# An encoder layer in split fp32: work moved at the stage borders, and a new slot order in the mixer

## Chip, cores and metric

The kernel runs on one core of one Trainium2 chip. The metric is the device time of one execution in microseconds; the time before is the median of three runs. Engines: PE is TensorE (matrix products), DVE is VectorE, ACT is ScalarE, POOL is GpSimd, SP is the engine that issues most DMAs.

## What is computed

One layer of a streaming encoder on 1088 tokens (1024 of a prompt, 64 of a sample with caches), width 1024, all in fp32:

```python
x = x + 0.5 * swiglu_ffn(x, *ffn1)              # rms norm, 1024 -> 2 x 2816 -> 1024
h = rms_norm(x, mix_g)
o_a, o_b, state = mixer(h)                      # projections, two kinds of attention
x = x + merge_branches(h, o_a, o_b, *merge_w)   # gates, two projections, one out
x = x + 0.5 * swiglu_ffn(x, *ffn2)
x = x + per_layer_embedding(x, pe, *ple)        # "PLE"
```

Branch a of the mixer attends over a band of chunks, with a bias by relative position looked up in a table, and a sink for each head. Branch b attends causally with a decay: the scores of a query and a key get the difference of cumulative sums of log_sigmoid(forget gate). The forget gates are 8 columns of the projection.

## The kernel before

Every product is made of three: an operand is split into a high part (rounded by ACT, names in `_hi`) and a low part (the difference, subtracted by DVE or POOL, names in `_lo`), and PE adds hi x hi, lo x hi and hi x lo in PSUM (`three`, L674 for most). So a piece of weights goes DMA (`_raw`), ACT (`_hi`), DVE (`_lo`), PE.

Everything is written out by hand: each engine has its own program, engines meet at semaphores, and an instruction waits for all that stands ahead of it on its engine.

- **Prologue.** SP loads x. ACT squares the first half's tiles (L1400), PE sums them over partitions (`first_stats`, L773), ACT takes roots (`half_roots`, L1131), DVE inverts (`half_inverse`, L1517) and makes the operands (`operand_step`: `b_raw` L1528, then `h_lo` and `b_lo`, L1536 and L1539, behind ACT's `operand_hi`, L1139 to L1142). The position biases go another way: PE looks the table up (`rel_table_rows`, L764), ACT copies it (`table_rel`, L1403) and writes it to memory (`rel_by_position`, L1405), and SP loads it again in eight pieces, `rel_rows` (L2134).
- **FFN.** The tokens are taken in two passes of 544. A pass has 11 groups of hidden columns. Its first two groups are plain products, in pieces of 128x512 (`plain_hi` L616, `plain_lo` L621), the other nine go in pairs by a Strassen scheme: POOL's `combine` (L1966 to L1977) makes sums of weight blocks, `block_hi` (L602) and `block_lo` (L610) split them, and `differences` on DVE (L1545 to L1550) makes the matching sums of operands once a pass. `gate_part` and `other_part` on DVE (`steps`, L1579 to L1605) put the quarters together. `group_out` multiplies by the out weights (`out_hi` L635, `out_lo` L639: w_hi and w_lo, 128x1024), and DVE adds to x (`add_half`, L1612). Between head and last group a loop runs 8 periods of about 33 us.
- **The norm of the second half** is prepared while the first pass runs: ACT squares its 8 tiles (`half_square`, L1197), POOL sums them (`half_sums`, L1988), both in the head of the pass.
- **Border to the mixer (or to PLE).** Norms are applied in chunks of 364, 364 and 360 tokens, in `NORM_ORDER` (`norm_hi` L1109, `norm_lo` L1488), between the additions of the last group; the next stage's weights are split by `split_lo` (L588).
- **Mixer.** After a first pair of units (`unit_pair`), `mix` runs slots: 6 dense ones, then one for each of 76 attention items (20 of branch a, 56 of branch b). `unit_products` (L902) are the projections, 24 products of 128x364 for a unit and chunk; `scores` (L932), `turns` (L951: probabilities are transposed on PE) and `values_product` (L975) belong to an item, and run in different slots: `LAG` sets how many slots lie between an item's scores and its turn, and its values follow one slot later. ACT's `exponents` (L1345), `copies` (`probs_t`, L1294) and `outputs` (`o_t`, L1359) and DVE's row maxima (`neg_top`, L1771) and weights lie between. `log_forget` (ACT L1363 to L1368, DVE L1806 to L1817) turns forget gates into cumulative sums. `head_sums` (L993) and `turned_values` (L1005) serve norms of heads and values.
- **Merge.** Four groups, each with `unit_out` (outputs (m, c): tile m, token chunk c); the last feeds the norm of FFN2 (`merge_sums` on POOL, L1999).

The heart of a mixer slot on PE:

```python
scores(g, ...)
unit_products(taken, taken + todo // 2)
values_product(g, ...)
head_sums(slot, use[1])
unit_products(taken + todo // 2, taken + todo)
turns(TURN_AT[slot])
turned_values(slot, use[2], use[3])
```

## Time and profile before

| | |
|---|---|
| time, median of 3 runs | 2606.1 us (2605.12 to 2611.69) |
| the profiled execution | 2604.11 us, span 2602.4 us |
| mean granted clock of PE | 0.987 |
| busy: PE, DVE, ACT, POOL | 2525.6, 1817.5, 1011.1, 778.8 us |
| FFN1, both passes | about 20 to 795 us of the span |
| mixer, merge | about 795 to 1300, 1300 to 1694 us |
| FFN2, PLE | about 1694 to 2470, 2470 to 2602 us |

Times in the profile are microseconds from the span's start. "Busy" is time in which an engine executes; "idle before" stands in brackets behind an instruction, with what ended it. PEclk is the clock granted to PE, 1.00 at full speed.

### The profile page before, as it was taken

What the parts mean: (1) busy time and instruction counts of PE and PEld (TensorE: products, weight loads), DVE (VectorE), ACT (ScalarE), POOL (GpSimd) and SP (SyncE); (2) the same over time, 40 slices, a digit from 0 to 9 for tenths busy, and PEclk for the clock granted to TensorE, in tenths of its full rate; (3) what the DMA queues carried; (4) which work ended last, traced back from release to release, by engine and by line L of the source; (5) the groups of instructions that cost most, each with busy time, mean ns of one, the idle gap of its engine ahead of it and who ended that gap; (6) DMA issues with size and microseconds to landing.
All of it is one profiled execution on the core that took longest, in us unless ns stands there. A gap on an engine that the chain in (4) does not pass through costs nothing.

```text
span 2602.4 us, 47124 instructions
## 1 busy us (share of the span) xinstructions
PE 2525.6 (97%) x18062; PEld 2374.9 (91%) x18062; DVE 1817.5 (70%) x3345; ACT 1011.1 (39%) x1911; POOL 778.8 (30%) x628
## 2 busy tenths in 40 slices
PE   7999999999998899999999999989999999999899
PEld 7999999999998787777789889889999899999899
DVE  6688888788878676555433434487888777888764
ACT  5333343333335675555421111243333333333431
POOL 2355541455443000111100000234554224555410
PEclk8999999999999999999999999999999999999999
DMA  4222222222224101221121111122222222222112
GB/s 178 97 89 91 98 86 94 91 92 94 98 72 147 56 30 34 68 72 46 43 109 41 42 41 48 57 74 90 98 98 91 80 82 98 98 98 98 66 41 93
DMA packets 61846, 209.39 MB, mean 80 GB/s; under 512 B 7968, under 2 KB 10440, under 8 KB 61536
## 3 DMA queue, kind: packets, MB, share of 16 engines
q1 hardware_dynamic: 61408, 206.64, 22.2%
q8 instruction: 144, 2.36, 0.4%
q14 instruction: 38, 0.31, 0.0%
q10 hardware_dynamic: 256, 0.08, 0.0%
HBM read 192.11 MB, written 16.15 MB: 80 GB/s over the span
## 4 chain that ended last, share of the span: by engine, by line
PE 90%; DVE 6%; ACT 2%; issue 1%; DMA 0%; POOL 0%; DVEq 0%; ACTq 0%; POOLq 0%; SPq 0%
PE psum L674 68%; PE psum L902 9%; PE psum L1064 5%; PE psum L932 2%; PE psum L975 2%; PE psum L951 2%; PE psum L993 1%; DVE w_lo L639 1%; DVE rstd L1517 1%; DVE h_lo L1488 0%; DVE x L1612 0%; DVE w_lo L588 0%; DVE rstd L1495 0%; DVE b_raw L1528 0%; PE psum L773 0%
## 5 line engine op out<-in xcount | busy, mean ns | idle before, releaser
L674 PE MATMUL psum<-hid_hi,w_hi 128*128 128x272 f32 (+2 forms) x1536 | 451.7, 294 | 4.9 <-DVE hid_lo L1510 4.9
L674 PE MATMUL psum<-hid_lo,w_hi 128*128 128x272 f32 (+2 forms) x1536 | 451.8, 294 | 0.0
L674 PE MATMUL psum<-hid_hi,w_lo 128*128 128x272 f32 (+2 forms) x1536 | 451.2, 294 | 0.0
L674 PE MATMUL psum<-h_hi,gate_hi 128*128 128x272 f32 x1200 | 351.1, 293 | 27.2 <-DVE b_lo L1536 12.6
L674 PE MATMUL psum<-h_hi,other_hi 128*128 128x272 f32 x1200 | 351.5, 293 | 13.9 <-DVE other_lo L610 13.9
L674 PE MATMUL psum<-h_hi,other_lo 128*128 128x272 f32 x1200 | 350.4, 292 | 0.0
L674 PE MATMUL psum<-h_hi,gate_lo 128*128 128x272 f32 x1200 | 349.8, 292 | 0.0
L674 PE MATMUL psum<-h_lo,other_hi 128*128 128x272 f32 x1200 | 348.7, 291 | 0.0
L674 PE MATMUL psum<-h_lo,gate_hi 128*128 128x272 f32 x1200 | 348.2, 290 | 0.0
L1612 DVE SCALAR_TENSOR_TENSOR x<-psum,x 128x272 f32<-128x272 f32 x736 | 290.9, 431 | 59.1 <-PE psum L674 57.8
L674 PEld LDWEIGHTS psum<-hid_hi,w_hi 128*128 128x128 f32 x1536 | 289.2, 188 | 6.6 <-issue 6.3
L2004 POOL TENSOR_TENSOR hid_lo<-prod,hid_hi 128x272 fp32r<-128x272 f32 x160 | 140.3, 903 | 501.8 <-ACT hid_hi L1167 342.7
L674 PEld LDWEIGHTS psum<-hid_lo,w_hi 128*128 128x128 f32 x1536 | 290.1, 189 | 0.4
L674 PEld LDWEIGHTS psum<-hid_hi,w_lo 128*128 128x128 f32 x1536 | 289.6, 189 | 0.0
L674 PEld LDWEIGHTS psum<-h_hi,gate_hi 128*128 128x128 f32 x1200 | 228.3, 190 | 28.8 <-DVE gate_lo L621 10.2
L674 PEld LDWEIGHTS psum<-h_hi,other_hi 128*128 128x128 f32 x1200 | 229.3, 191 | 14.9 <-DVE other_lo L610 14.9
L674 PEld LDWEIGHTS psum<-h_lo,other_hi 128*128 128x128 f32 x1200 | 229.7, 191 | 0.0
L674 PEld LDWEIGHTS psum<-h_hi,other_lo 128*128 128x128 f32 x1200 | 229.2, 191 | 0.0
L674 PEld LDWEIGHTS psum<-h_lo,gate_hi 128*128 128x128 f32 x1200 | 228.8, 191 | 0.1
L674 PEld LDWEIGHTS psum<-h_hi,gate_lo 128*128 128x128 f32 x1200 | 228.4, 190 | 0.0
L610 DVE TENSOR_TENSOR other_lo<-other_raw,other_hi 128x1024 fp32r<-128x1024 f32 (+1 forms) x144 | 213.7, 1491 | 0.0
L674 PE MATMUL psum<-h_hi,w_hi 128*128 128x364 f32 (+1 forms) x576 | 193.7, 336 | 5.7 <-DVE h_lo L1488 3.8
(224 smaller groups left out, 5560.5 us busy)
## 6 DMA issues: line engine op xcount, KB each, us to landing
w_raw<-w_units SPq DMA_DIRECT2D x149, 512.0 KB, 3.2
gate_raw<-w_units SPq DMA_DIRECT2D x88, 512.0 KB, 4.2
other_raw<-w_units SPq DMA_DIRECT2D x88, 512.0 KB, 4.2
x<-x_t SPq DMA_DIRECT2D x16, 272.0 KB, 6.8
x_saved<-x SPq DMA_DIRECT2D x8, 544.0 KB, 6.1
x<-x_saved SPq DMA_DIRECT2D x8, 544.0 KB, 7.9
y_out<-x SPq DMA_DIRECT2D x8, 544.0 KB, 4.6
f_keys<-f_cumulative SPq DMA_DIRECT2D x4, 1024.0 KB, 6.6
```

Source lines behind the costliest of these rows:

```text
L610: dve.tensor_tensor(pair_lo[slot][:, first:first + n, :], pair_raw[slot][:, first:first + n, :], pair_hi[slot][:, first:first + n, :].bitc ...
L639: dve.tensor_tensor(w_lo[:, j, :], w_raw[:, j, :], w_hi[:, j, :].bitcast(F32), ALU.subtract).then_inc(out_lo_done, 1)
L674: mm = pe.matmul(out, w, m, start=first and n == 0, stop=last and n == 2)
L902: mm = pe.matmul(psum[:, x % 2, 0:width], (w_hi, w_hi, w_lo)[way][:, slot, k * P:(k + 1) * P], (h_hi, h_lo, h_hi)[way][:, k, c0:c0 + width ...
L932: mm = pe.matmul(psum[0:rows, SC[h], at:at + width], q[hb:hb + HD, part["b"] * P:part["b"] * P + rows], keys, start=True, stop=True)
L951: mm = pe.transpose(out, cols, ident[0:rows, 0:rows])
L975: mm = pe.matmul(psum[hb:hb + HD, PV, col:col + rows], vals[0:width, hb:hb + HD], probs_t[0:width, h, j * P:j * P + rows], start=first, st ...
L993: pe.matmul(psum[:, ST, 0:n], blocks, head_sq[:, r % 2, 0:n], start=True, stop=True).then_inc(head_sum_full, 1)
L1064: mm = pe.matmul(psum[:, ev.mod(BANKS), 0:n], w_raw[:, slot, (4 * br + k) * P:(4 * br + k + 1) * P], o_t[:, 4 * br + k, c0:c0 + n], start= ...
L1517: dve.reciprocal(rstd[:, c0:c0 + HN], rstd[:, c0:c0 + HN]).then_inc(half_rstd_done, 1)
L1612: dve.scalar_tensor_tensor(x[:, m, c0:c0 + HN], bank(e + n), half, x[:, m, c0:c0 + HN], ALU.mult, ALU.add).then_inc(psum_free, 1)
L2004: pool.tensor_tensor(part(lo, n), part(prod2, n), part(hi, n).bitcast(F32), ALU.subtract).then_inc(hid2_lo_done, 1)
```

## The change

1. **Prologue.** ACT loads the table of square roots ahead of the inputs by a dummy root. The table look-up moves behind the statistics on PE; the copy `table_rel` moves among the operand copies on ACT, and the write `rel_by_position` behind the last of them. `plain_lo` is done in two parts, behind operand steps 0 and 4.
2. **Heads.** The 8 squares and sums of the second half move from the head into the loop's periods (two in the first, one in each of six more), on ACT and POOL; their loops are unrolled in pass 0.
3. **Last pair of a pass.** Its second combine moves from POOL to DVE, ahead of `gate_part`; out weights of the last two groups use three slots and are split behind `block_lo`.
4. **Borders.** `NORM_ORDER` and the places of `norm_lo` and `split_lo` among the 32 additions change; at the mixer's and PLE's start three `inverse` go ahead of the reads.
5. **Mixer slots.** Scores, values and turns stand ahead of the unit products; lags grow from 1 to 2 (a) and 2 to 3 (b).
6. **Forget gates.** Their 8 low columns are copied beside the 8 high ones, so one product serves hi x hi and hi x lo; 16 instead of 24 products for a chunk, and the halves are added on DVE.
7. **Merge.** Outputs of groups 0 to 2 come in the order (0,0), (0,1), (1,0), (1,1), (0,2), (1,2) and on; in the last group the weights of FFN2 are split earlier, and the first three operand steps lie among the additions.

```diff
-LAG = {"a": 1, "b": 2}
+LAG = {"a": 2, "b": 3}
...
-NORM_ORDER = [(m, 0) for m in TILE_ORDER[:5]] + [(m, c) for m in TILE_ORDER[:5] for c in (1, 2)] + \
-    [(m, c) for m in TILE_ORDER[5:] for c in range(NCH)]
+NORM_ORDER = [(0, 0), (1, 0), (0, 1), (0, 2), (2, 0), (1, 1), (1, 2), (5, 0), (2, 1), (2, 2), (6, 0)] + \
+    [(m, c) for m in (5, 6) for c in (1, 2)] + [(m, c) for m in TILE_ORDER[5:] for c in range(NCH)]
...
+OUT_SLOTS = {2: (1, 2), 1: (0, 1)}
...
             def unit_products(q0, q1):
...
+                    both = MIX_UNITS[n][0] == "f"
+                    if both and way == 2:
+                        continue
...
             def mix():
...
-                    unit_products(taken, taken + todo // 2)
                     if slot in VALUE_AT:
...
+                    if slot in TURN_AT:
+                        turns(TURN_AT[slot])
+                    unit_products(taken, taken + todo // 2)
...
-                    if slot in TURN_AT:
-                        turns(TURN_AT[slot])
...
             def ffn(stage):
-                def period(number, group, e):
+                def period(number, group, e, tiles=()):
...
+                    for m in tiles:
+                        half_square(number, m)
...
-                    if t == 0:
-                        for m in range(4):
-                            half_square(number, m)
                     plain_sigmoid(group, e)
-                    if t == 0:
-                        for m in range(4, KD):
-                            half_square(number, m)
...
+            act.wait_ge(set_up, 2)
+            act.activation(eps_root[:], eps[:], ACT.Sqrt)
...
             for k in range(KD):
                 operand_hi(0, k)
+                if k == 1:
+                    act.wait_ge(table_full, 1)
+                    act.activation(table_rel[:], psum[0:8, 5, 0:REL], ACT.Copy, scale=-1.0).then_inc(table_done, 1)
+            act.wait_ge(table_done, 1)
+            act.dma_start(rel_dram, table_rel[:]).then_inc(table_out, 16)
             act.wait_ge(table_out, 16)
...
-                    out_lo(dve, At(last - 1), 0)
-                    out_lo(dve, At(last - 1), 1)
+                    sq = strassen_pair(At(2 * last + 1), number)
+                    dve.wait_ge(combined, 4 * sq.base)
+                    combine(dve, sq, At(last), 1)
                     gate_part(At(last), number, At(el))
                     for n in range(4):
                         block_lo(dve, At(2 * last + 1), number, 1, n)
+                    out_lo(dve, At(last - 1), 0, 2)
+                    out_lo(dve, At(last - 1), 1, 2)
+                    out_lo(dve, At(last), 0, 1)
...
-                norm_lo(norm, 0)
-                split_lo(dve, At(follower["u"]), At(follower["s"]))
-                norm_lo(norm, 1)
-                done = 2
-                for n in range(16):
-                    add_half(1, At(el + 30), n, 0.5)
...
+                done = 0
+                for n in range(32):
+                    add_half(1, At(el + 14 + 16 * (n // 16)), n % 16, 0.5)
+                    if n == 14:
+                        out_lo(dve, At(last), 1, 1)
+                    if n == 23:
+                        split_lo(dve, At(follower["u"]), At(follower["s"]))
+                    if n in (12, 20, 26, 29):
                         norm_lo(norm, done)
                         done += 1
...
+            def f_low_beside(n):
...
+                dve.tensor_copy(hi, lo).then_inc(f_beside, 1)
...
             def mix(e):
+                for c in range(NCH):
+                    inverse(0, c)
                 for c, (c0, n) in enumerate(CH):
-                    inverse(0, c)
                     read_scaled(k0[:, c0:c0 + n], e + c, c, 0)
...
             half_inverse(0)
             for n in range(len(OPERAND_STEPS)):
                 operand_step(0, n)
-                if n == 1:
-                    plain_lo(dve, 0, 0)
+                if n in (0, 4):
+                    plain_lo(dve, 0, 0, range(n // 2, n // 2 + 2))
```

ACT in the prologue, the kernel before: the table's copy and its write stand between the squares of the statistics, and a table load stands ahead of the roots.

```order
L1400 ACT_TABLE_LOAD
...
L1400 ACTIVATE sq_a<-x 128x544 [waits x_in0_1]
...
L1403 ACTIVATE table_rel<-psum 8x384 [waits table_full]
L1405 DMA rel_by_position<-table_rel 8x384 [waits table_done]
L1400 ACTIVATE sq_a<-x 128x544 [waits sq_a_read,x_in0_6]
...
L1131 ACT_TABLE_LOAD [waits half_stat_full]
...
L1131 ACTIVATE rstd<-psum,eps 128x272 [waits half_stat_full]
```

The same in the changed kernel, from the roots on (`h_hi` and `b_hi` are the operand copies):

```order
L1165 ACTIVATE rstd<-psum,eps 128x272 [waits half_stat_full] x2
L625 ACTIVATE gate_hi<-gate_raw 128x512 [waits gate_in]
...
L1438 ACTIVATE table_rel<-psum 8x384 [waits table_full]
...
L1176 ACTIVATE h_hi<-b_raw 128x2x272 [waits scaled] x4
L1440 DMA rel_by_position<-table_rel 8x384 [waits table_done]
L625 ACTIVATE other_hi<-other_raw 128x512 [waits other_in,table_out]
```

The write has moved behind all operand copies, and ACT waits for its end before it copies the next weights; the second table load is gone from here. SP's order is the same in both kernels: the `rel_rows` loads wait for that write, and the out weights stand behind them.

DVE at the border of a pass, before and then in the changed kernel (`other_raw` holds the weight blocks that are combined, `steps` and `gate` the quarters):

```order
L1517 RECIPROCAL rstd<-rstd 128x272 x2
L639 TENSOR_TENSOR w_lo<-w_raw,w_hi 128x1024 x2
L1579 TENSOR_TENSOR steps<-steps,psum 128x272
...
L1597 TENSOR_TENSOR gate_130<-gate_130,prod_131 128x272 x4
L610 TENSOR_TENSOR other_lo<-other_raw,other_hi 128x1024 x3
...
L621 TENSOR_TENSOR gate_lo<-gate_raw,gate_hi 128x512 x4
```

```order
L1548 RECIPROCAL rstd<-rstd 128x272 x2
L662 TENSOR_TENSOR other_raw<-other_raw 128x512
...
L1610 TENSOR_TENSOR steps<-steps,psum 128x272
...
L1628 TENSOR_TENSOR gate_130<-gate_130,prod_131 128x272 x4
L619 TENSOR_TENSOR other_lo<-other_raw,other_hi 128x1024 x3
...
L655 TENSOR_TENSOR w_lo<-w_raw,w_hi 128x1024 x3
L631 TENSOR_TENSOR gate_lo<-gate_raw,gate_hi 128x512 x4
```

Four combinations (one is shown) stand where two w_lo stood, and three w_lo now stand between other_lo and gate_lo.

PE in the mixer, one slot before and one in the changed kernel (`k`, `q`: scores; `probs_t`: values; `probs`: turns; `w_hi`, `w_lo`: unit products, of which the first is shown):

```order
L932 MATMUL psum<-k_98,q_97 128x256 x4
L902 MATMUL psum<-h_lo,w_hi 128x360
...
L975 MATMUL psum<-probs_t,v_tok_102 64x128 x8
L993 MATMUL psum<-head_sq,consts 128x364
L902 MATMUL psum<-h_hi,w_hi 128x364
...
L951 MATMUL psum<-consts,probs 128x128 x8
```

```order
L966 MATMUL psum<-ak_t,q_97 64x128 x2
L966 MATMUL psum<-k_98,q_97 64x64 x2
L1009 MATMUL psum<-probs_t,v_tok_102 64x128 x8
L985 MATMUL psum<-consts,probs 128x128 x8
L936 MATMUL psum<-h_hi,w_lo 128x364
...
L1027 MATMUL psum<-head_sq,consts 128x364
L936 MATMUL psum<-h_lo,w_hi 128x364
```

Values and turns have moved ahead of all products of the slot.

## Rows read from the trace of the kernel before

**Rows 1.** The page: busy time by engine, and one line of its DMA part.

```profile
PE 2525.6 (97%) x18062; PEld 2374.9 (91%) x18062; DVE 1817.5 (70%) x3345; ACT 1011.1 (39%) x1911; POOL 778.8 (30%) x628
...
w_raw<-w_units SPq DMA_DIRECT2D x149, 512.0 KB, 3.2
```

**Rows 2.** Windows: length, busy PE, PEld, DVE, ACT, POOL; clock, DMA share, GB/s.

```profile
20.00:55.00 35.00, 26.31 (x193) 26.12 (x194) 29.76 (x46) 20.61 (x38) 12.12 (x8) 0.89 0.38 130
55.00:350.00 295.00, 295.00 (x2331) 295.00 (x2331) 245.41 (x408) 108.86 (x175) 147.51 (x104) 0.99 0.26 92
...
1020.00:1300.00 280.00, 278.37 (x2004) 213.70 (x2002) 147.60 (x412) 150.83 (x350) 38.37 (x68) 1.00 0.17 55
...
1680.00:1730.00 50.00, 39.84 (x277) 39.23 (x278) 39.48 (x63) 25.52 (x44) 14.06 (x11) 0.91 0.18 64
...
1727.90:1731.00 3.10, 3.10 (x14) 3.10 (x15) 3.10 (x7) 3.10 (x6) 0.46 (x1) 0.50 0.02 5
```

**Rows 3.** Waits of PE: line, releaser; us in total, times, longest.

```profile
PE psum L674 <- DVE other_lo L610: 13.9, 4, 4.0
...
PE psum L1005 <- ACT v_tok L1308: 3.5, 1, 3.5
...
PE psum L932 <- DVE neg_top L1771: 2.1, 1, 2.1
PE psum L993 <- DVE k L1504: 2.0, 1, 2.0
...
PE psum L902 <- DVE q L1724: 1.7, 1, 1.7
PE psum L975 <- ACT probs_t L1294: 1.6, 3, 0.7
```

**Rows 4.** Timeline of PE: start, us, instruction, [idle before, its releaser]; prologue and heads.

```profile
9.46 0.81 PE L764 MATMUL psum<-onehot,table 32*8 32x384 f32 x2
...
24.05 0.57 PE L674 MATMUL psum<-h_hi,gate_hi 128*128 128x272 f32 x1 [9.81 <-DVE b_lo L1536]
...
54.78 0.39 PE L674 MATMUL psum<-h_hi,gate_hi 128*128 128x272 f32 x1 [4.63 <-DVE gate_lo L621]
...
1727.86 0.59 PE L674 MATMUL psum<-h_hi,gate_hi 128*128 128x272 f32 x1 [5.13 <-DVE gate_lo L621]
```

**Rows 5.** Timeline of ACT, prologue.

```profile
13.87 1.28 ACT L1131 ACT_TABLE_LOAD   x1 [1.23 <-PE psum L773]
15.17 0.86 ACT L1131 ACTIVATE rstd<-psum,eps 128x272 f32<-128x272 f32 x2
...
31.55 0.66 ACT L1142 ACTIVATE h_hi<-b_raw 128x544 fp32r<-128x544 f32 x1 [0.67 <-DVE b_raw L1528]
```

**Rows 6.** Timeline of DVE: heads, pass borders, a lone w_lo.

```profile
20.76 2.49 DVE L621 TENSOR_TENSOR gate_lo<-gate_raw,gate_hi 128x512 fp32r<-128x512 f32 x4
...
42.22 4.60 DVE L639 TENSOR_TENSOR w_lo<-w_raw,w_hi 128x1024 fp32r<-128x1024 f32 x2 [2.20 <-ACT w_hi L635]
46.74 2.44 DVE L1545 TENSOR_TENSOR t_raw<-b_raw 128x1088 f32<-128x1088 f32 x1
49.11 1.28 DVE L1546 TENSOR_TENSOR t_raw<-b_raw 128x1088 f32<-128x1088 f32 x1
...
398.62 1.23 DVE L639 TENSOR_TENSOR w_lo<-w_raw,w_hi 128x1024 fp32r<-128x1024 f32 x1
...
1715.31 2.29 DVE L639 TENSOR_TENSOR w_lo<-w_raw,w_hi 128x1024 fp32r<-128x1024 f32 x1 [2.44 <-ACT w_hi L635]
...
2040.20 4.21 DVE L639 TENSOR_TENSOR w_lo<-w_raw,w_hi 128x1024 fp32r<-128x1024 f32 x2
```

**Rows 7.** Timeline of SP's queue, prologue.

```profile
15.87 5.04 SPq L2134 DMA_DIRECT2D rel_rows<-rel_by_position  x8
```

**Rows 8.** DMA issues up to 60 us: count, KB each, us to landing.

```profile
w_raw<-w_units SPq DMA_DIRECT2D x2, 512.0 KB, 7.7
```

**Rows 9.** Window of the mixer's dense slots, unit products (L902) alone.

```profile
846.00:853.00 7.00, 6.68 (x36) 6.05 (x36) 1.00 0.01 2
```

More of the change, by code:

```diff
@@ L102 @@
 PRODUCTS = 3 * KD
+F_LOW = 32
 def attention_items():
@@ L616, in plain_hi, with plain_lo @@
                 act.activation(pair_hi[slot][:, b, :], pair_raw[slot][:, b, :], ACT.Copy).then_inc(pair_hi_done, 1)
-        def plain_lo(dve, group, slot):
-            for n, b in enumerate(PLAIN_BLOCKS):
+        def plain_lo(dve, group, slot, part=range(4)):
+            for n in part:
+                b = PLAIN_BLOCKS[n]
                 dve.wait_ge(pair_hi_done, 4 * (2 * group + slot) + n + 1)
@@ L720, in unit_pair, with unit_out @@
                         stats(norm, STAT_STEPS[step])
-            def unit_out(u, s, e, rows, h_count):
+            def unit_out(u, s, e, rows, h_count, order=tuple((m, c) for m in range(4) for c in range(NCH))):
                 pe.wait_ge(w_lo_done, (s + 1).v)
@@ L848, in pair, with group_out @@
                     mm.then_inc(psum_full, 1)
-            def group_out(group, e, hi, lo):
+            def group_out(group, e, hi, lo, ahead=0):
                 for j in range(2):
+                    slot = OUT_SLOTS.get(ahead, (0, 1))[j]
                     pe.wait_ge(out_lo_done, 2 * group + j + 1)
@@ L1262, in ffn @@
                     if t == 0:
-                        out_hi(act, At(last), 0)
-                        operand_hi(number + 1, 0)
-                        out_hi(act, At(last), 1)
-                        for k in range(1, KD):
+                        out_hi(act, At(last), number, 1, 1)
+                        act.wait_ge(psum_full, el + 30)
+                        for k in range(KD):
                             operand_hi(number + 1, k)
@@ L1373, in mix @@
                 for slot in range(N_SLOTS):
-                    if slot - 1 in TURN_AT:
-                        copies(TURN_AT[slot - 1])
+                    if slot in VALUE_AT:
+                        outputs(VALUE_AT[slot])
+                    if slot in TURN_AT:
+                        copies(TURN_AT[slot])
                     late, use = ST_AT.get(slot - 1), ST_AT.get(slot)
@@ L1384, in mix @@
                         head_root(use[1])
-                    if slot in VALUE_AT:
-                        outputs(VALUE_AT[slot])
                     for n in range(3, len(MIX_UNITS)):
@@ L1647, in ffn @@
                         head_gains()
-                    out_lo(dve, At(group), 0)
-                    out_lo(dve, At(group), 1)
+                    for j in range(2):
+                        out_lo(dve, At(group), j)
                     differences(number, e)
@@ L1680, in ffn @@
                     for n in range(16):
+                        add_half(t, At(el + 14), n, 0.5)
+                    for n in range(16):
                         add_half(t, At(el + 30), n, 0.5)
-                        if n == 5:
-                            out_lo(dve, At(last), 1)
+                        if n == 2:
+                            out_lo(dve, At(last), 1, 1)
                         if n % 2:
@@ L1926, in _ @@
                         split_lo(dve, u + 1, s + 1)
+                    if half == m == 0:
+                        for c in range(NCH):
+                            inverse(1, c)
                     for c, (c0, n) in enumerate(CH):
-                        if half == m == 0:
-                            inverse(1, c)
                         read_scaled(ple_gate[:, m, c0:c0 + n], e + c, c, 1 if half == m == 0 else None)
@@ L2007, in ffn, with period @@
             def ffn(stage):
-                def period(number, group):
-                    combine(group.times(2) + 1, number, group, 1)
-                    combine((group + 1).times(2), number, group + 1, 0)
+                def period(number, group, tiles=()):
+                    sq = strassen_pair(group.times(2), number)
+                    combine(pool, sq + 1, group, 1)
+                    combine(pool, sq + 2, group + 1, 0)
+                    for m in tiles:
+                        half_sum(number, m)
                     hidden2_lo(group, quarter, hid2_hi, hid2_lo)
@@ L2104, in ffn @@
                     el = e + E_LAST
+                    ev, where = el - E_PERIOD, at + 16 + 6 * (LOOP - 1)
+                    sp.wait_ge(psum_full, ev + 7)
+                    load_pair(0, At(where))
+                    if t == 0:
+                        sp.wait_ge(sum_b_done, KD * (stage["first"] // 2 + 1))
+                    load_out(1, At(where + 5), OUT_SLOTS[2][1])
+                    sp.wait_ge(psum_full, ev + 15)
+                    load_out(0, At(at + U_FFN - 2), OUT_SLOTS[1][0], last_in)
+                    sp.wait_ge(psum_full, ev + 23)
+                    load_out(0, At(where + 4), OUT_SLOTS[2][0])
+                    sp.wait_ge(psum_full, ev + 30)
+                    load_pair(1, At(where + 1))
                     sp.wait_ge(psum_full, el + 7)
```

212 lines of the change are left out of this document (109 added, 103 removed).

## The prediction

> **What bounds the kernel now.** I read the page first: TensorE (PE) is busy for 2525.6 of 2602.4 us, 97% [rows 1], so a change pays only where it removes PE idle time, PE work, or PE time at the lower clock. Then the windows by stage: in the loop of a feed-forward stage (FFN) PE is busy for all of 295.00 us, and in the settled mixer, 1020 to 1300, for 278.37 of 280 [rows 2]. Those have nothing to give. The two FFN heads have: 26.31 of 35 and 39.84 of 50 us, with a granted clock of 0.89 and 0.91 where a loop has 0.99 [rows 2]. The waits of PE say for whom it stands: other_lo, v_tok, neg_top, q, k, probs_t [rows 3] and, at the heads, b_lo and gate_lo [rows 4]. The clock I price from a row: in the 3.10 us behind the wait that ends at 1727.86 it is 0.50, the 1.2 of 2.4 GHz [rows 2, 4]; half of such a stretch, some 1.6 us, is lost beside the wait itself.
>
> The sum is made against the profiled execution, 2604.1 us, which lies 2.0 below the median of 2606.1. A measurement can tell about 0.3% (7.8 us) from no change.
>
> **1. Prologue and head of FFN1: 3.4 us gained, bounds -0.7 and 9.6.** ACT loads a table for 1.28 us between the last statistics product and the roots [rows 5]; the load moves ahead of the inputs, where ACT waits anyway: 1.28. Two table products, 0.81 us, leave PE's queue ahead of the statistics [rows 4]: 0.8. DVE subtracts four weight pieces in 2.49 us before the first operand [rows 6]; two of them now go later: 1.2. So PE starts at 24.05 - 3.3 = 20.8.
>
> But the head ends at another wait: PE stands for 4.63 us until 54.78, for gate_lo [rows 4], which DVE reaches after two out-weight subtractions (w_lo), 4.60, four differences, 2.44 for the first and 1.28 for each after it, and then the gate_lo themselves [rows 6]. POOL's sums of squares ran beside the first three of these; a lone w_lo takes 1.23 us [rows 6], so each loses 1.07 there. With the sums moved into the loop the chain shortens by 2 x 1.07 + 1.16 = 3.3, and the start by 3.3 as well: the wait could go whole, 3.3 + 4.63 + 1.6 of clock = 9.5, and with a tenth for ACT's shorter queue 9.6, the upper bound.
>
> I don't take it, for what is moved on a queue. The table of biases by position, whose copy and write ACT issued between two squares, now leaves behind ACT's last operand copy, which ended at 31.55 + 0.66 = 32.2 [rows 5] and would end 3 us sooner, near 29. SP, which waits for it, issued eight rel_rows loads from 15.87 on, in 5.04 us [rows 7], with the out weights behind them. Before, SP was let go at 15.87; now at 29 plus the write, for which I count between 2 us and the 5 that a load took under traffic: 32. Then the out weights are issued at 37 and land, at 3.2 us [rows 1] to 7.7 [rows 8], between 40 and 45; ACT rounds them in 1 us each and DVE starts w_lo at about 43, where it started at 42.22 [rows 6]. From there 2.5 (two w_lo) + 5.1 (four differences) + 1.9 (three of four gate_lo) gives 52.5; as the differences need no weights but stand behind w_lo, nothing overtakes. With loads at 42 it is 51.4, my value (the lower landing time is that of 149 such loads): 3.4 gained on 54.78. If they land last, 55.5: 0.7 lost.
>
> On the table load the Trainium skill (ScalarE: Activation LUTs, "What ACT_TABLE_LOAD costs") gives another price: 1283 ns and a drain of some 1380 ns more at each switch. Here the roots begin at 15.17, 0.02 us after the load's end [rows 5]; by the page the forecast would be 1.4 us lower, and I go by the row.
>
> **2. Head of FFN2: 6.7 gained, bounds 3 and 7.5.** The same chain without rel_rows: PE waits 5.13 us until 1727.86 [rows 4], and DVE's w_lo start at 1715.31, at 2.29 for one [rows 6], behind an ACT that squares four tiles first. Without the sums the w_lo save 2.1 and the first difference 1.16; without ACT's four squares, at the 0.66 that a copy of the same 128x544 takes at most [rows 5], the start saves about 2.2 (they overlap a little): 5.5 against 5.13. So the wait just goes, with its 1.6 of clock. The margin is small; half a wait left gives the lower bound.
>
> **3. Pass borders: 0.4 in FFN1, 2.5 in FFN2 (bounds 0 and 5).** DVE takes reciprocals, then two w_lo (4.21 us at 2040.20 [rows 6]), then the steps for which PE waits. The change puts four 128x512 combinations there, at the 0.62 of a gate_lo piece (2.49 / 4 [rows 6]) some 2.6 to 2.9 with their order kept, and w_lo behind other_lo's subtractions: 1.3 off the steps of FFN2, half a microsecond at FFN1, where the two ran shorter. The wait for other_lo that follows (of the four, 13.9 us [rows 3], two lie here) moves along. In FFN2 both waits lie close and share a slow stretch, of which I give back 1.2.
>
> **4. FFN1 to the mixer, 1.3 (bounds 0 and 6); FFN2 to the last stage, 3.5 (0 and 6).** The other two waits for other_lo, nearly 4 us each [rows 3], lose 0.5 by a combine on DVE instead of POOL. Behind them lie short waits for x, w_lo and h_lo. The order spreads h_lo among the additions, but DVE's work there remains: I keep most of the waits at the first border and drop half at the second.
>
> **5. Mixer start: 3.3 gained, bounds 0 and 7.** The 2.0 for k [rows 3] goes, as three reciprocals precede the reads. The forget gates take 16 products a chunk instead of 24: 24 fewer at 6.68 us for 36 [rows 9], 4.4. Against it: the early items wait for v_tok 3.5, neg_top 2.1 and q 1.7 [rows 3], where ACT and DVE work through the forget gates' logarithm and scans. Values and turns at the slot's head meet these chains with half a slot less of products in front: I count 4.2 + 0.6 + 4.0, 1.5 more, and one more slow stretch, 1.6. What is added for the forget gates (a copy, a longer addition) runs on DVE beside products.
>
> **6. Settled mixer, tail and merge: 0.5.** PE's only waits there are 1.6 us in three for probs_t [rows 3], at the tail, where no products are left: 0.2. The lag grows by one slot while values move up by half of one, so a chain has half a slot more than before. Of the reordered merge outputs the first two stay in place, and so the wait for the second's input: 0. The last merge group overlaps more of the next norm: 0.3.
>
> **Sum:** 3.4 + 6.7 + 0.4 + 2.5 + 1.3 + 3.5 + 3.3 + 0.5 = 21.6. 2604.1 - 21.6 = 2582.5; with the 2.0 to the median **2584.5 us**.
>
> **The rivals.**
> - *More goes than I count, 0.17.* The out weights land before DVE needs them (9.6 for 3.4), and the two borders out of the FFN hide their waits (5 more): 21.6 + 6.2 + 5 = 32.8, **2573**. For it: 3.2 us to landing on a free queue. Against: SP's 5.04 us of issue.
> - *The borders don't move, 0.15.* DVE bounds them, and another order of its work changes which output is late, not the last. Then 4.4 of products, 5 of FFN2's head, 2 of the prologue and 1 remain: 12.4, **2594**.
> - *POOL's sums hurt in the loop, 0.05.* If each of eight sums costs a DVE subtraction beside it what a w_lo loses, 1.07, a pass loses 8.6, and two 17 of the 21.6: **2601**. It decides only where DVE is just in time; over the loop it is busy for 245.41 of 295 [rows 2]. The Trainium skill (GPSIMD Engine Reference, "8. Key points") says that GpSimd shares its SBUF interfaces with VectorE, in contention with instructions of two SBUF inputs; by that rule the sums charge DVE wherever they are put, and the trace agrees for w_lo.
> - *Slower: the slot heads of the mixer wait, 0.05.* Turn, ACT's copy, value product: if this chain sets the pace, each of 76 item slots waits as the tail does, 1.6 / 3 = 0.54 [rows 3]: 41 us, **2625**. It decides from 21.6 / 76 = 0.28 us a slot. Against: the third slot of lag.
>
> **How the numbers follow.** My sum has 0.58, the rivals the rest. The range reaches from past the first rival, one border more, 2568, to past the second, with half of FFN2's head, 2598. Faster by over 0.3% means below 2598.3: my sum, the first rival and nearly all of the second, 0.87; within 0.3% 0.08, the third and the second's end; slower 0.05.
>
> **What would show it.** Right: no PE wait near 1722 and no slow stretch behind it; still some 4 us of waiting for gate_lo before the third group of FFN1, now near 51, with the out weights issued near 37; 24 fewer forget products; waits of about 4 us at the first value items. Wrong: PE waits in each slot after 1020, waits for other_lo above 4 us, idle time in the loops.

## The result, and the profile after

| | before | after |
|---|---|---|
| median of the runs, us | 2607.96 (2605.12 to 2611.69, 4 runs) | **2567.09** (2566.22 to 2568.53, 4 runs) |
| after / before | | **0.9843** [0.9826, 0.9860] |
| profiled execution, us | 2604.11 | 2568.53 |
| its span, us | 2602.4 | 2566.7 |

The gain is 40.9 us by the medians, where 21.6 were forecast, and the time lies 0.9 us below the range. Between the two profiled executions it is 35.7 on the spans: that of before ran 3.9 under its median, that of after 1.4 over. The parts below are counted on the spans.

The page of after, busy time by engine [rows 1]. The unit products are 24 fewer, and PE's busy time fell by 21.6 us:

```profile
PE 2504.0 (98%) x18038; PEld 2364.9 (92%) x18038; DVE 1797.5 (70%) x3362; ACT 1010.5 (39%) x1912; POOL 768.9 (30%) x612
```

Where the span was shortened, by landmarks on PE's timeline: the first product after the wait in question, for the mixer its first unit product (823.21 before, 819.81 after), and for the pass border of FFN2 the end of the last product ahead of it. The lengths and the busy time of PE are those of windows between the landmarks:

| stretch | before, us | after, us | gain | PE idle, before to after |
|---|---|---|---|---|
| start to first FFN1 product | 24.05 | 21.91 | 2.1 | |
| to the third group of FFN1 | 30.73 | 32.53 | -1.8 | 4.6 to 6.0 |
| to the pass border's end (other_lo) | 321.08 | 319.74 | 1.3 | 5.2 to 4.0 |
| to the first unit product of the mixer | 447.35 | 445.63 | 1.7 | 9.0 to 7.1 |
| to the first merge product | 477.54 | 463.02 | **14.5** | 11.6 to 12.8 |
| to the first product of FFN2 | 396.07 | 395.30 | 0.8 | 10.2 to 9.4 |
| to the pass border of FFN2 | 345.13 | 338.31 | 6.8 | 5.1 to 0 |
| over this border | 8.82 | 5.81 | 3.0 | 6.0 to 4.0 |
| to the end | 551.63 | 544.45 | 7.2 | 14.3 to 11.3 |

The fifth row is the surprise: the mixer gained most, and PE stands idle *longer* there than before, although the wait for k (2.0 of the 11.6) is gone from it.

Windows of after, in the columns of [rows 2] (the last one is the stretch behind the wait for v_tok):

```profile
20.00:55.00 35.00, 27.08 (x194) 26.86 (x195) 25.61 (x45) 16.97 (x29) 0.00 (x0) 0.84 0.42 137
55.00:350.00 295.00, 295.00 (x2335) 295.00 (x2334) 241.99 (x410) 112.47 (x184) 166.11 (x112) 1.00 0.28 95
1000.00:1280.00 280.00, 277.62 (x2044) 218.56 (x2044) 150.39 (x423) 154.06 (x364) 40.41 (x70) 1.00 0.18 55
...
859.50:862.90 3.40, 3.40 (x16) 2.26 (x15) 1.65 (x7) 1.73 (x9) 0.00 (x0) 0.50 0.00 0
```

Read the third row against [rows 2]. Both windows end within 3 us ahead of the first merge product, and PE is busy for as long as before in 280 us, but with 2044 products instead of 2004. The same work is denser, which no column of busy time shows. In the first row the clock is 0.84: the wait in the head of FFN1 has its slow stretch still.

Waits of PE in after, in the columns of [rows 3]:

```profile
PE psum L702 <- DVE other_lo L619: 12.6, 4, 3.1
PE psum L702 <- ACT table_rel L1438: 6.9, 1, 6.9
PE psum L702 <- DVE gate_lo L631: 6.0, 1, 6.0
PE psum L702 <- DVE h_lo L1519: 5.9, 8, 1.9
...
PE psum L1039 <- ACT v_tok L1337: 4.5, 1, 4.5
PE psum L966 <- DVE neg_top L1802: 3.8, 2, 3.5
PE psum L702 <- DVE b_lo L1567: 2.4, 1, 2.4
...
PE psum L702 <- DVE steps L1610: 1.8, 2, 0.9
PE psum L1009 <- ACT probs_t L1323: 1.6, 3, 0.7
```

The wait for k has shrunk from 2.0 to 0.6, that for q is gone, v_tok and neg_top have grown, and gate_lo stands once, at 6.0, in the head of FFN1 alone. Timeline of PE at the heads and borders, as in [rows 4]:

```profile
21.91 0.59 PE L702 MATMUL psum<-h_hi,gate_hi 128*128 128x272 f32 x1 [6.93 <-ACT table_rel L1438]
...
54.44 0.60 PE L702 MATMUL psum<-h_hi,gate_hi 128*128 128x272 f32 x1 [6.01 <-DVE gate_lo L631]
...
1678.13 0.39 PE L702 MATMUL psum<-h_hi,gate_hi 128*128 128x272 f32 x1 [2.36 <-DVE b_lo L1567]
...
2017.32 0.39 PE L702 MATMUL psum<-h_hi,gate_hi 128*128 128x272 f32 x1 [0.88 <-DVE steps L1610]
...
2022.25 0.39 PE L702 MATMUL psum<-h_hi,other_hi 128*128 128x272 f32 x1 [3.15 <-DVE other_lo L619]
```

And the chain that ends in the wait of 54.44, from the queue it starts on. ACT writes the table of biases late; SP, which waits for it, then issues eight row loads ahead of the out weights; ACT rounds these when they land, and DVE follows [rows 5 to 8]. Timelines of ACT, of SP's queue and of DVE:

```profile
30.21 0.52 ACTq L1440 DMA_DIRECT2D rel_by_position<-table_rel  x1
...
44.01 1.06 ACT L650 ACTIVATE w_hi<-w_raw 128x1024 fp32r<-128x1024 f32 x1 [7.25 <-DMA w_raw<-w_units]
```

```profile
31.61 5.04 SPq L2181 DMA_DIRECT2D rel_rows<-rel_by_position  x8
36.69 1.06 SPq L2110 DMA_DIRECT2D w_raw<-w_units  x2
```

```profile
45.10 2.55 DVE L655 TENSOR_TENSOR w_lo<-w_raw,w_hi 128x1024 fp32r<-128x1024 f32 x2 [7.55 <-ACT w_hi L650]
47.56 1.28 DVE L1576 TENSOR_TENSOR t_raw<-b_raw 128x1088 f32<-128x1088 f32 x1
...
52.50 2.49 DVE L631 TENSOR_TENSOR gate_lo<-gate_raw,gate_hi 128x512 fp32r<-128x512 f32 x4
```

The two w_lo take 2.55 us where they took 4.60 beside POOL's sums [rows 6], and the differences 1.28 each: the work shrank as counted. But DVE begins it 2.9 us later than before, as it stood 7.55 us for ACT, and ACT for the weights.

### The profile page after: what moved, and what is told of

It is laid out like the page before. It is cut to its first block, busy times and chain, and to the rows that moved or that the text cites. A ratio compares the mean times of both kernels' runs of the same rounds, so it can differ in the third digit from the quotient of the medians.

```text
span 2566.7 us, 46461 instructions
## 1 busy us (share of the span) xinstructions
PE 2504.0 (98%) x18038; PEld 2364.9 (92%) x18038; DVE 1797.5 (70%) x3362; ACT 1010.5 (39%) x1912; POOL 768.9 (30%) x612
## 4 chain that ended last, share of the span: by engine, by line
PE 90%; DVE 6%; ACT 2%; issue 1%; DMA 1%; POOL 0%; SPq 0%; DVEq 0%; ACTq 0%; POOLq 0%
PE psum L702 70%; PE psum L936 8%; PE psum L1098 5%; PE psum L966 2%; PE psum L1009 2%; PE psum L985 2%; DVE h_lo L1519 1%; PE psum L1027 1%; DVE rstd L1548 0%; ACT probs L1374 0%; DVE x L1643 0%; DVE probs L1802 0%; DMA w_raw<-w_units 0%; DVE b_raw L1559 0%; PE psum L799 0%
## 5 line engine op out<-in xcount | busy, mean ns | idle before, releaser
L2036 POOL TENSOR_TENSOR hid_lo<-prod,hid_hi 128x272 fp32r<-128x272 f32 x160 | 155.6, 999 | 562.6 <-ACT hid_hi L1201 324.9
L619 DVE TENSOR_TENSOR other_lo<-other_raw,other_hi 128x1024 fp32r<-128x1024 f32 (+1 forms) x144 | 202.2, 1411 | 0.0
```

What stands on the lines that cost most here:

```text
L619: dve.tensor_tensor(pair_lo[slot][:, first:first + n, :], pair_raw[slot][:, first:first + n, :], pair_hi[slot][:, first:first + n, :].bitc ...
L2036: pool.tensor_tensor(part(lo, n), part(prod2, n), part(hi, n).bitcast(F32), ALU.subtract).then_inc(hid2_lo_done, 1)
```

## The experiments

All are edits of the changed kernel; ratios are to the kernel before, measured beside them. "Below" and "above" compare with the change's 0.9843.

**The order in the mixer's slot.** The change moves turns and values ahead of the unit products and lets the lag grow by a slot. The first run undoes both:

```diff
-LAG = {"a": 2, "b": 3}
+LAG = {"a": 1, "b": 2}
...
+                    unit_products(taken, taken + todo // 2)
                     if slot in VALUE_AT:
...
-                    if slot in TURN_AT:
-                        turns(TURN_AT[slot])
-                    unit_products(taken, taken + todo // 2)
...
+                    if slot in TURN_AT:
+                        turns(TURN_AT[slot])
...
```

ACT's outputs and copies go back to their old places as well.

> The changed kernel with the old mixer order and the old lags (scores, half the products, values, the other half, turns). Theory A: each slot then has one more change from unit products to short products and back, about 0.14 us, and 76 slots cost 10.8; the early waits and slow clock of the new order go (some 4.9). Sum +5.9: 2573. Rival B: the settled mixer takes the same time in either order and the gain came from elsewhere (forget gates, early part): -4.9, 2562.

Measured: 2577.25 us, 0.9886 [0.9869, 0.9902], 11 us above the change (by the ratios, as below where nothing else is said). So the slots are a real part of the gain, and a larger one than the whole 0.2 that the prediction gave them. The traces agree: from the scores of item 6 to the last scores this run takes 390.2 us, as before the change, and the change takes 379.3. Two more runs take them apart: the old lag alone (only the LAG line above), and the old order with the new lag (all but that line).

> The changed kernel in its new slot order with the old lags 1 and 2. Theory A: the order pays and the lag only gives slack: with one slot less, turns stand one slot behind their scores, and PE waits for probabilities in the slots of branch a, where the chain of DVE and ACT is some 5 us of a slot of 6.6; under 0.5 us in 20 slots, 2570. Rival B: without the third slot of lag most slots wait 0.3 to 1 us: 2590 to 2620.

> The changed kernel in the old slot order with the new lags 2 and 3. Theory A: items 20 to 70 take 269.2, as before the change and with the old lags; 2575 to 2577. Rival B: part of the gain is the lag's, 265 or less for these items, 2571.

Measured: 2569.3 (0.9853 [0.9836, 0.9869]) and 2582.49 (0.9905 [0.9888, 0.9921]). What tells is the same work in each trace: the stretch from the scores of item 20 to those of item 70, 50 slots. Windows of before, of after, of the old order with the new lag, and of the new order with the old lag:

```profile
1002.20:1271.50 269.30, 269.30 (x1901) 206.52 (x1900) 143.14 (x387) 145.52 (x330) 36.83 (x62) 1.00 0.19 61
```

```profile
991.30:1253.30 262.00, 260.43 (x1903) 204.98 (x1902) 141.36 (x385) 142.97 (x328) 37.01 (x62) 1.00 0.20 61
```

```profile
997.20:1266.50 269.30, 269.30 (x1905) 207.15 (x1904) 143.58 (x387) 145.52 (x330) 36.78 (x62) 1.00 0.19 61
```

```profile
990.20:1256.70 266.50, 260.83 (x1899) 204.44 (x1898) 141.52 (x385) 142.43 (x328) 36.92 (x62) 1.00 0.18 60
```

| items 20 to 70 | length, us | PE busy | waits |
|---|---|---|---|
| before | 269.3 | 269.3 | 0 |
| old order, old lag | 269.3 | 269.3 | 0 |
| old order, new lag | 269.3 | 269.3 | 0 |
| new order, old lag | 266.5 | 260.8 | 5.7 |
| the change | 262.0 | 260.4 | 1.6 |
| turns at the slot's end | 270.2 | 261.1 | 9.1 |
| values between the halves (second try) | 294.8 | 268.9 | 25.9 |
| sums ahead of all products | 262.0 | 258.7 | 3.3 |

PE's time follows the order alone: 8.9 us in 50 slots, 0.18 a slot, with the clock at 1.00 and the same products. The lag buys no PE time; with the new order it takes 4.1 us of waits away. With the old order there was no wait for it to take. In the time of the whole kernel the lag is not shown to pay: the old lag lies 2.2 us above the change by the medians, with intervals that overlap, and the early waits are shorter with it (2.3 for v_tok and 0.9 for neg_top instead of 4.5 and 3.8). (The 7 us by which the old order with the new lag lies above the old order with the old one on the spans are not in these slots. Some 4 stand ahead of the mixer, where the programs are the same: clock 0.90 for 0.93 in the first 50 us, and 0.99 for 1.00 between 380 and 819. The rest, 3.9, is in the first six items and behind the last scores.)

Where the 0.18 comes from can be read off PE's timeline. Two slots with the same products (10 unit products, 4 for scores, 16 for values, 8 turns), without sums and without a wait; first before, 5.01 us from scores to scores (rows left out are unit products, 0.16 to 0.17 us from one to the next):

```profile
1253.18 1.13 PE L932 MATMUL psum<-k,q 64*128 64x512 f32 x4
1254.24 0.43 PE L902 MATMUL psum<-h_hi,w_lo 128*128 128x364 f32 x1
1254.51 0.33 PE L902 MATMUL psum<-h_hi,w_hi 128*128 128x364 f32 x1
...
1255.01 0.33 PE L902 MATMUL psum<-h_hi,w_hi 128*128 128x364 f32 x1
1255.27 1.09 PE L975 MATMUL psum<-probs_t,v_tok 128*64 128x128 f32 x16
1256.29 0.43 PE L902 MATMUL psum<-h_lo,w_hi 128*128 128x364 f32 x1
1256.56 0.33 PE L902 MATMUL psum<-h_hi,w_lo 128*128 128x364 f32 x1
...
1257.06 0.33 PE L902 MATMUL psum<-h_hi,w_lo 128*128 128x360 f32 x1
1257.23 1.04 PE L951 MATMUL psum<-consts,probs 128*128 128x128 f32 x8
1258.19 0.49 PE L932 MATMUL psum<-k,q 64*128 64x256 f32 x2
```

and after, 4.76 us:

```profile
1235.61 1.13 PE L966 MATMUL psum<-k,q 64*128 64x512 f32 x4
1236.66 1.09 PE L1009 MATMUL psum<-probs_t,v_tok 128*64 128x128 f32 x16
1237.69 1.09 PE L985 MATMUL psum<-consts,probs 128*128 128x128 f32 x8
1238.54 0.41 PE L936 MATMUL psum<-h_hi,w_lo 128*128 128x364 f32 x1
1238.79 0.32 PE L936 MATMUL psum<-h_hi,w_hi 128*128 128x364 f32 x1
...
1240.11 0.33 PE L936 MATMUL psum<-h_hi,w_lo 128*128 128x360 f32 x1
1240.37 0.49 PE L966 MATMUL psum<-k,q 64*128 64x256 f32 x2
```

Before, PE breaks off the unit products in mid-slot for the values. The first value starts 0.26 behind the last unit product, where the next unit product would have started after 0.17; and when PE comes back, the second unit product starts 0.27 behind the first, again for 0.17. That is 0.09 + 0.10 = 0.19 for one interruption, by start times in both traces. In after, the values stand in one block with scores and turns, and this interruption is gone; one is left in each slot. The other 0.05 or so lies within the block: turns hold PE for 0.85 ahead of a unit product and for 0.96 ahead of scores, but going from unit products to scores takes 0.26 where going to turns took 0.17. These times are short against the busy times in the table of groups, and nothing in it names them.

Slots with sums gain less. Of the 50, 18 hold a pair of head sums, and in 15 of these the sums of after start 0.23 to 0.60 us behind the unit product, not 0.17 as in the run with the turns at the slot's end (below): they wait for ACT's square, 3.7 us in all, of which the table counts 1.6 as waits. So by their lengths the 32 slots without sums are 6.5 us shorter than before, and the 18 with sums 0.7.

**Values back between the halves**, twice: in PE's queue alone, then with ACT's outputs moved behind its exponents to suit.

```diff
+                    if slot in TURN_AT:
+                        turns(TURN_AT[slot])
+                    unit_products(taken, taken + todo // 2)
                     if slot in VALUE_AT:
...
-                    if slot in TURN_AT:
-                        turns(TURN_AT[slot])
-                    unit_products(taken, taken + todo // 2)
```

> The changed kernel with only the value products back between the two halves of the unit products; turns, scores and lags as changed. Theory A (changes between kinds of products on PE): +10.8, 2578, without any new waits of PE. Rival B (it is the lag or the turns' place that pays): 2567, no change.

> The changed kernel with only the value products back between the two halves of the unit products, and on ACT the output copies back behind the head squares and exponents, so that these don't wait for the values; turns, scores and lags as changed. Theory A (changes between kinds of products on PE): PE stays busy through the settled mixer, yet needs 0.17 us more a slot, +13: 2580. Rival B (the place of the turns or the lag pays): within 2 of the changed kernel, 2567. A third, that ACT is late again: waits for head_sq or probs_t in each slot, over 2600.

Measured: 2640.8 (1.0127 [1.0110, 1.0144]) and 2629.7 (1.0089 [1.0072, 1.0106]), both slower than before. PE's time in the settled slots of the second is nearly back at 268.9 (some 1.5 to 2 of it at the lower clock: 0.99 over the window), so the values' place, that is the second interruption in a slot, carries most of the 0.18. The rest of the loss is a wait, in 34 slots of the whole mixer:

```profile
PE psum L1027 <- ACT head_sq L1348: 49.1, 34, 1.8
```

The timelines of ACT and PE show where it comes from:

```profile
929.62 1.09 ACT L1323 ACTIVATE probs_t<-psum 128x512 f32<-128x512 f32 x2 [3.63 <-PE psum L1009]
930.59 0.51 ACT L1348 ACTIVATE head_sq<-k 128x364 f32<-128x364 f32 x1
```

```profile
928.48 1.09 PE L1009 MATMUL psum<-probs_t,v_tok 128*64 128x128 f32 x16
931.24 0.85 PE L1027 MATMUL psum<-head_sq,consts 128*128 128x364 f32 x2 [1.67 <-ACT head_sq L1348]
```

ACT copies the turned probabilities of one item into the tile from which the values of the item before are still read. With values in mid-slot this copy stands for 3.63 us, and the square that the sums need stands behind it in ACT's queue. So the new place of the values does two things: it groups PE's work, and it frees that tile before ACT wants it.

**Turns at the slot's end**, ACT's copies in the next slot; values stay ahead:

```diff
-                    if slot in TURN_AT:
-                        turns(TURN_AT[slot])
                     unit_products(taken, taken + todo // 2)
...
+                    if slot in TURN_AT:
+                        turns(TURN_AT[slot])
```

> The changed kernel with the turns at the slot's end, so that they stand right ahead of the next slot's scores and values; on ACT their copies come in the next slot, as before. The number of changes between unit products and short products is that of the changed kernel. Theory A (the number of changes sets PE's time in a slot): items 20 to 70 take 262, as in the changed kernel, if the copies are there in time; 2567. Rival B (the turns' place at the slot's head pays): 269 as before the change, 2575. If values wait for the copy of a turn that stands directly ahead of them: 76 x 0.5 or more, over 2600.

Measured: 2584.92, 0.9922 [0.9905, 0.9939], 21 above the change. PE's own time stays (261.1); it waits instead:

```profile
PE psum L1009 <- ACT probs_t L1323: 17.1, 30, 1.9
```

30 waits for the copy, 0.57 us each, where after has three. It is the price that the prediction's slower rival set for one (0.54), in a slot that has only the scores between turns and values; but 30 of the 76 slots wait, not all. With one interruption in a slot, PE's time is that of the change although the turns stand elsewhere. The change's order avoids it.

**Sums ahead of all unit products**, with ACT's square first in the slot:

```diff
-                    unit_products(taken, taken + todo // 2)
                     use = ST_AT.get(slot)
                     if use and use[0] == "sums":
                         head_sums(slot, use[1])
+                    unit_products(taken, taken + todo // 2)
```

> The changed kernel with the sums of head squares also ahead of the unit products (39 of the slots have them), the square first on ACT. Theory A: one change between kinds of products less in 39 slots, 0.1 to 0.17 us each: -4 to -6.5, 2562. Rival B: the square is not there at the slot's head, PE waits 0.5 us or more in 39 slots: +20, 2587.

Measured: 2577.03, 0.9884 [0.9868, 0.9901], 11 above. The gain that was expected did not come. In 50 slots PE is busy for 1.7 us less and waits for as much more, 262.0 in all as with the change. The loss lies ahead of them: in the dense slots before the first item, 30.0 us for 24.5, PE waits for the squares of the norms:

```profile
826.93 0.88 PE L1027 MATMUL psum<-head_sq,consts 128*128 128x364 f32 x2 [1.07 <-DVE y_sq L1766]
...
```

**The row loads behind the third load of the head**, on SP's queue; the wait and the loop move as they are:

```diff
+                        if stage is FFN1 and t == 0 and done == 12:
+                            sp.wait_ge(table_out, 16)
+                            for h in range(8):
...
-            sp.wait_ge(table_out, 16)
-            for h in range(8):
...
```

> The changed kernel with the eight rel_rows loads moved on SP behind the weight loads of the second half of the head. Theory A (the 6.0 us wait for gate_lo in FFN1's head comes from out weights that stand behind rel_rows): w_lo begins near 38 instead of 45.1, the wait shrinks to under 1 us and its slow clock goes: -6 to -9, 2559. Rival B (the gate weights themselves land late, or DVE's chain is the bound): a wait of 3 us or more remains, 2564.

Measured: 2557.57 (2552.60 to 2558.78), 0.9813 [0.9797, 0.9830], 9.5 below the change by the medians, 7.8 by the ratios (the intervals just touch; no run of the one lies within the runs of the other, and the wait is gone from the trace). With the wait for the table out of its way, SP issues the out weights at 12.79 instead of 36.69, they are there when DVE reaches them, and PE starts the third group without a wait. SP's queue, DVE and PE of this run:

```profile
12.79 1.12 SPq L2110 DMA_DIRECT2D w_raw<-w_units  x2
...
59.83 5.04 SPq L2129 DMA_DIRECT2D rel_rows<-rel_by_position  x8
```

```profile
36.29 2.36 DVE L655 TENSOR_TENSOR w_lo<-w_raw,w_hi 128x1024 fp32r<-128x1024 f32 x2
```

```profile
46.68 0.29 PE L702 MATMUL psum<-h_hi,gate_hi 128*128 128x272 f32 x1
```

The third group starts 7.8 us earlier than in after. The queue was the bound of the head, as the prediction had it, and the head now gains 8.1 on before in this trace, most of the upper bound of 9.6 that the prediction kept for weights in time.

**Forget gates with 24 products a chunk**: `both = False`, eight rows for 40, no copy beside, a plain addition of the bias.

> The changed kernel with 24 products a chunk for the forget gates, as before, and no copy beside. Theory A: 24 products at 0.186 more on PE's path, +4.4: 2571.5. Rival B: the chain of ACT and DVE behind the forget gates sets the early mixer and hides some of them: +1 or less, 2568.

Measured: 2570.13, 0.9860 [0.9843, 0.9876]: 4.4 above by the ratios, 3.0 by the medians, for products counted at 4.4; the intervals overlap. In the traces the stretch from the first unit product to the first scores takes 27.7 us instead of 24.5. The early waits give some back: 4.2 for v_tok and 2.8 for neg_top instead of 4.5 and 3.8.

**The forget gates' logarithm three slots later** (slot DENSE + 3 on ACT, as many later on DVE and SP; ACT also waits for its result once):

> The changed kernel with the forget gates' logarithm on ACT and the scans on DVE three slots later (the first output of the second pair waits for the saved sums). Theory A: the early waits for v_tok 4.5 and neg_top 3.5 come from that work standing in front of the first items, which have no lag yet; later it is covered by the lag: -8 and up to 3 of slow clock, 2557 to 2559. Rival B: the same waits come back as waits for probs_t or neg_top three slots on: 2566 to 2568.

Measured: 2564.39, 0.9840 [0.9824, 0.9856], no difference from the change. The waits for v_tok and neg_top went, but for 0.4, and others came:

```profile
PE psum L1027 <- ACT head_sq L1348: 8.9, 8, 5.3
```

**The old order of the norms at the pass ends:**

```diff
-NORM_ORDER = [(0, 0), (1, 0), (0, 1), (0, 2), (2, 0), (1, 1), (1, 2), (5, 0), (2, 1), (2, 2), (6, 0)] + \
...
+NORM_ORDER = [(m, 0) for m in TILE_ORDER[:5]] + [(m, c) for m in TILE_ORDER[:5] for c in (1, 2)] + \
...
```

> The changed kernel with the old NORM_ORDER at both borders (places among the additions as changed). Theory A: bringing all three chunks of tile 0 early pays at the borders; the old order brings back waits for h_lo of some 3 us at each, +6: 2573. Rival B: what pays is that the norms are spread among the additions and the weights split behind them: within 1.5 of 2567.

Measured: 2573.4 (2566.93 to 2574.50), 0.9866 [0.9850, 0.9883], 6 above, with intervals that overlap by a little. In place of after's eight short waits for h_lo (5.9 in all) stand two long ones, at the ends of the two FFN stages:

```profile
PE psum L702 <- DVE h_lo L1519: 11.2, 2, 5.9
```

So the order of the norms is worth 5.3 us of waiting. That they are spread among the additions is the same in this run and was not tried by itself.

**The best of these together**: the row loads late, as above, and the logarithm behind the first copy of v_tok on ACT with DVE's scans one slot later.

> The changed kernel with rel_rows behind the head's loads, and in the mixer the forget gates' logarithm behind the first copy of v_tok on ACT, the scans on DVE in two parts in two slots. Theory: 2557.6 of rel_rows alone, less 4.4 of the wait for v_tok and 2 of the 3.5 for neg_top: 2551, and up to 3 less where the slow clock behind these waits goes too. Rival: the waits move to the next user of ACT, as with the later logarithm: 2556.

Measured: **2554.02** (2553.57 to 2556.45), 0.9799 [0.9783, 0.9815], 52 us under before. The long wait of the early items is now one for q, 5.4 us, and 3.5 in six for head_sq: moved once more. Against the late row loads alone it is 3.5 lower with intervals that overlap, so of the two only the row loads are shown to pay.

## Why the prediction was right in sign and too small

By the spans 35.7 us were gained where the sum has 21.6. Of the 14.1 more, 11.0 lie in the mixer (parts 5 and 6), 4.1 at the borders out of the FFN, 1.9 at the pass borders and in the merge; the head of FFN1 gave 3.1 less than forecast. That the time lies only 0.9 us below the range is in part luck: this shortfall hides part of the miss in the mixer.

**Part 6, the settled mixer, is the step that failed.** It counted the chains (half a slot more for each, and no wait to lose: both true) and put 0.2 on them. It never asked what the *order* costs on PE itself where PE doesn't wait. The window of [rows 2] showed PE busy for 278 of 280 us, and the prediction read that as "nothing to give". Busy time contains the changes between kinds of products. From the scores of item 6 to the last scores PE needs 99.7 + 269.2 + 21.2 us before (cut at items 20 and 70) and 97.0 + 262.0 + 20.3 in after, 10.9 less; the run with the old slots takes as long as before, and lies 11.2 above the change by the ratios. Behind the last scores 1.2 us come back, as the longer lag leaves more of the last items' work there.

**Part 5, the mixer's start**, gave 4.8 for 3.3 by its lengths. From the first unit product to the first scores 5.4 us went, from 29.9 to 24.5. The 24 products are 4.0 of them, at 0.166 from start to start (the 6.68 for 36 of [rows 9] counts ends that overlap, hence the forecast's 4.4). The rest is the wait for k of 2.0, in whose place one of 0.5 for head_sq stands; another for k, 0.6, stands ahead of the first unit product. The early waits were forecast as 4.2 + 0.6 + 4.0 and measured as 4.45 for v_tok, 0.35 and 3.47 for neg_top; none for q appears. The clock was under-counted: over the first six items (50.0 us in after, 49.4 before) it is 0.90 for 0.97, so 5.0 us are lost for 1.5, where one stretch of 1.6 more was counted. Against that, these six slots hold 22 products fewer by the records, as turns and values come a slot later.

**Part 4, the borders out of the FFN**, gave 1.7 and 7.2 for 1.3 and 3.5. The waits for other_lo there went from 3.96 and 3.69 to 3.14 each, the half microsecond that was taken. Before, PE's FFN products stood 10.9 us in all for w_lo, h_lo and x, now 6.4 for h_lo and w_lo, and PE's idle time fell by 1.9 and 3.0, near the forecast. What it left out is the clock behind these waits at the second border: 4.2 of the 7.2 are PE busy for less time with the same 3954 products, at a mean clock of 0.99 for 0.98. The traces of eleven runs above have the change's program in this stretch and take 541.5 to 545.9 us there, the one of before 551.6; so the gain is there, and its size differs from run to run. The run with the old norms shows what turns on the order: with it, 11.2 us for h_lo alone, about what w_lo, h_lo and x took before the change. That it is the last h_lo of PE's *next* group that counts, and that spreading brings this one forward, is how the traces read; it wasn't tried by itself.

**Part 1, the head of FFN1**, forecast 3.4 of a range from -0.7 to 9.6 and measured 0.3. Mechanism and place are as written: PE starts earlier, SP issues the rows at 31.61 for 32 and the out weights at 36.69 for 37, DVE starts w_lo late, and a gate_lo wait stands at the third group. Mis-sized is the landing: 7.6 us, the upper row of the two prices, so DVE began at 45.1, and the wait ended at 54.4 and not 51.4. (The 51.4 is not what its own rows give: 37 + 3.2 to landing + 1 on ACT + 9.5 of chain is 50.7, its 43 makes 52.5, and the upper price 55.2 instead of 55.5.) The start at 21.9 and not 20.8 lies in part, by 0.45, in a wait that was not foreseen: PE's operands end at 21.40, but its first FFN1 product now stands for the copy of the bias table on ACT (table_rel), which ends at 21.85.

**Part 2** is right: 6.8 for 6.7, no wait for gate_lo in FFN2 and no slow stretch behind one. **Part 3**: 1.3 and 3.0 for 0.4 and 2.5; the waits for steps fell from 2.02 and 2.87 to 0.88 each, 1.1 and 2.0 less, and in FFN2 the rest is clock. **Merge**: 0.8 for 0.3. Parts 2 and 3, the merge's order and the earlier table load have no run of their own. From the first merge product to the end of FFN2's pass border the change and the runs above take 736.9 to 739.7 us, before 750.0, so the sum of merge, part 2 and FFN2's share of part 3 is well shown, and its split rests on the two traces. So does the price of the table load: no wait of the drain that the Trainium skill (ScalarE: Activation LUTs, "What ACT_TABLE_LOAD costs") adds to it is seen, as in after the dummy root starts at 3.45, 0.02 us after the end of the load that now lies there; no run here isolates it.

**The rivals.** "More goes than I count" was right in the main on the borders (4.1 more, where it has 5) and wrong on the out weights. "The borders don't move" is out. POOL's sums do not hurt in the loop: POOL is busy for 166.11 us there against 147.51, DVE for 241.99 against 245.41 [rows 2], and PE is busy for all of the 295. The Trainium skill (GPSIMD Engine Reference, "8. Key points") says that GpSimd shares its SBUF interfaces with VectorE, in contention with instructions of two SBUF inputs. The trace agrees for the w_lo pair, 2.55 us alone and 4.60 beside the sums; in the loop it cost PE nothing. The slower rival, a slot that waits for its own copy, did not come; the run with turns at the slot's end made that wait.

## What to carry to other kernels

A PE that is busy for the whole of a stretch can still be ordered badly: look at the time from start to start where one kind of product follows another, and put the short ones in one block, so that the long run is left and taken up again once. When a value moves on one engine, check which single tile the other engine reuses meanwhile, as its in-order queue turns one late copy into waits of things that have nothing to do with it. And ask of each late wait which load queue its first input came through; a late loop of loads ahead of it costs as much as the work saved.

## What the runs showed of the hardware that was not expected

- At a granted clock of 1.00, unit products follow each other at 0.166 us. Going from them to value products or scores takes 0.26 from start to start, to turns 0.18; on the return behind scores or values the second unit product starts 0.27 behind the first, behind turns 0.25 (means over items 20 to 70, before and after).
- The granted clock differs between executions of one program. The kernel with the late row loads has a mean clock of 0.993 at 2552.6 us, and of 0.991 at 2558.78: 6 us from run to run, where the change's own runs lie within 2.3. Differences under that size between two single executions say little.
